# A hybrid decoder layer on eight cores: one program for all sequence positions becomes three, values are turned by DMA, and rope is done without DMAs

## The reference, cut to what matters

```
h = rms_norm(x, norm_gain)                    # x: (2, 4096, 2048)
proj = einsum('bsd,de->bse', h, w_in)         # 16384 columns: q, k, v (3072 each), z_attn, u_pool, z_pool, gates
q = rms_norm(q per head); k = rms_norm(k per head)     # heads of 128
for g, (window, dilation) in enumerate(((128, 1), (512, 4), (2048, 16))):   # 8 heads each
    qg, kg = partial_rope(q[g]), partial_rope(k[g])    # the first 32 of 128 dims, half-split pairing
    # query t attends to t, t-d, ..., t-window
    o_g, lse_g = dilated_window_attention(qg, kg, v[g], window, dilation)
attn = sum over g of softmax(lse)[g] * o_g             # i.e. sum of numerators / sum of denominators
y_attn = (attn * silu(z_attn)) @ w_branch_attn
pooled_g = (causal_mean(u_g, 2|4|8|16) - u_g) @ pool_maps[g]
y_pool = (pooled * pool_scale * silu(z_pool)) @ w_branch_pool
x + (sigmoid(gates_a) * y_attn + sigmoid(gates_p) * y_pool) @ w_out
```

## Time and profile before

| | |
|---|---|
| median of 3 runs | 1629.32 us (1627.96 to 1629.89) |
| span of the profiled execution, slowest core | 1627.1 us |
| spans of the eight cores | 1618.4 to 1627.1 us |
| PE busy | 1519.9 us, 93% |
| DVE, ACT, POOL busy | 663.1, 531.4, 202.2 us |
| mean granted PE clock of a core | 0.970 to 0.977 |
| moved by DMA | 158.85 MB, 98 GB/s on average |

### The profile page before, as it was taken

How to read it: one execution, slowest core, us unless ns; L and a number is a source line. 1 busy time by engine, 2 the same in 40 slices (tenths; PEclk the granted TensorE clock), 3 DMA queues, 4 the chain that set the end, 5 groups by cost and what they waited for, 6 DMA issues and landing times.

```text
span 1627.1 us, 22823 instructions; the slowest of 8 cores (1618.4 to 1627.1 us)
## 1 busy us (share of the span) xinstructions
PE 1519.9 (93%) x7774; PEld 751.7 (46%) x7774; DVE 663.1 (41%) x976; ACT 531.4 (33%) x880; POOL 202.2 (12%) x191
## 2 busy tenths in 40 slices
PE   2638999899999999989999999999999999999997
PEld 0203434344655555445555555565444444444443
DVE  4356339732100476666116677676322222112221
ACT  2324345333211556655236665621111111111000
POOL 1535463300000100000000000000000000000000
PEclk9859999999999999999999999999999999999999
DMA  9951544114443644343343443445344444444883
GB/s 196 200 152 50 140 125 134 51 49 88 97 112 52 110 99 73 85 95 75 75 77 63 105 104 60 78 73 100 69 77 75 74 76 77 78 78 78 191 209 106
DMA packets 77874, 158.85 MB, mean 98 GB/s; under 512 B 33536, under 2 KB 41600, under 8 KB 76992
## 3 DMA queue, kind: packets, MB, share of 16 engines
q0 software_dynamic: 20592, 84.42, 30.9%
q1 hardware_dynamic: 56544, 72.51, 14.6%
q10 hardware_dynamic: 624, 0.46, 0.2%
HBM read 216.27 MB, written 20.97 MB: 146 GB/s over the span
## 4 chain that ended last, share of the span: by engine, by line
PE 85%; DMA 4%; DVE 3%; issue 2%; POOL 2%; ACT 2%; SPq 0%; ACTq 0%; DVEq 0%; POOLq 0%
PE ps L725 64%; PE ps L1431 7%; PE ps L1381 7%; POOL s_acc L660 2%; DMA s_rota_76<-s_kst_72 2%; PE ps L742 2%; PE ps L1067 2%; PE ps L1102 1%; DMA s_xs_59<-xc 1%; ACT s_sqf L658 1%; PE ps L1106 1%; PE ps L848 1%; DMA s_rotb_101<-s_qS_100 1%; DVE s_rota_78 L775 1%; DMA s_rota_76<-s_kst_69 1%
## 5 line engine op out<-in xcount | busy, mean ns | idle before, releaser
L725 PE MATMUL ps<-s_hX,s_w_56 128*128 128x512 bf16 (+3 forms) x3712 | 799.4, 367 | 0.0
L725 PEld LDWEIGHTS ps<-s_hX,s_w_56 128*128 128x128 bf16 x3712 | 363.6, 98 | 373.5 <-issue 3.5
L587 POOL DMA_DIRECT2D s_w_56<-wst x140 | 74.1, 533 | 1206.3 <-PE ps L725 918.2
L725 PE MATMUL ps<-s_w_56,s_hX 128*128 128x512 bf16 x672 | 147.2, 379 | 0.0
L1431 PE MATMUL ps<-s_mT,s_w_56 128*128 128x512 bf16 x512 | 110.7, 379 | 0.0
L725 PEld LDWEIGHTS ps<-s_w_56,s_hX 128*128 128x128 bf16 x672 | 71.6, 107 | 71.5
L660 POOL TENSOR_TENSOR s_acc<-s_acc,s_sqf 128x1024 f32<-128x1024 f32 x35 | 85.9, 2455 | 127.6 <-ACT s_sqf L658 127.6
L1431 PEld LDWEIGHTS ps<-s_mT,s_w_56 128*128 128x128 bf16 x512 | 50.1, 98 | 60.4
L746 ACT ACTIVATE s_rr_51<-ps 128x512 f32<-128x512 f32 (+1 forms) x72 | 41.4, 576 | 103.6 <-PE ps L742 69.9
L751 DVE SCALAR_TENSOR_TENSOR s_kS_105<-ps,s_cst,s_rr_51 128x384 bf16<-128x384 f32 x8 | 4.9, 614 | 171.8 <-PE ps L725 167.0
L725 PE MATMUL ps<-s_hTh_55,s_w_56 128*128 128x512 bf16 x256 | 66.7, 406 | 3.6 <-DVE s_hTh_55 L695 2.4
(11 more groups left out here) (286 smaller groups left out, 1513.9 us busy)
## 6 DMA issues: line engine op xcount, KB each, us to landing
s_w_56<-wst POOLq DMA_DIRECT2D x136, 512.0 KB, 5.2
s_w_56<-wst POOLq DMA_DIRECT2D x4, 2048.0 KB, 16.6
s_w_57<-wst POOLq DMA_DIRECT2D x2, 2048.0 KB, 23.2
s_xs_58<-xc SPq DMA_DIRECT2D x6, 512.0 KB, 4.7
s_xs_59<-xc SPq DMA_DIRECT2D x6, 512.0 KB, 5.9
s_xs_60<-xc SPq DMA_DIRECT2D x6, 512.0 KB, 6.5
s_xs_61<-xc SPq DMA_DIRECT2D x6, 512.0 KB, 6.7
s_xs_62<-xc SPq DMA_DIRECT2D x6, 512.0 KB, 7.6
```

The lines of the kernel that those rows point to most:

```text
L587: yield ("dma", "pool", size * 1048576, lambda g: g.dma_start(out=t[:].rearrange("p k n -> p (k n)"), in_=src), first, bufs, dsem)
L725: yield ("op", "pe", mm_us(n), lambda t, kc=kc, a=lhs(kc), b=rhs(kc): t.matmul(ps[i][:, 0:n], lhsT=a, rhs=b, start=(kc == 0), stop=(kc == ...
```

## The change

1. **Three programs.** The sequence of 4096 is cut into 1184, 1024, 944 and 944 tokens. Core 0 of a sequence runs program a (no halo, no stage 1), the next b (halo of 16x74 = 1184 tokens), the last two c (16x128 = 2048). All three lie in one binary. Each engine reads a number from DRAM and enters its program by `If`. Pieces of own tokens are 400, 400, 384 in a, 512, 512 in b, 480, 464 in c.
2. **Stage 1** takes only the halo, in chunks by residue modulo 16: 370, 222, 222, 370 in b and 512, 256, 256, 512, 512 in c. Own keys and values of group 2 are projected in the head loop as those of groups 0 and 1. The 16 key and value weight blocks of group 2 are therefore loaded twice in b and c.
3. **Values feature-major.** `values` projects like keys, ACT copies to `vT`, and `v_turn` turns 128x128 tiles into `v0`, `v1`, `v2` by a transposing DMA on SP (9 to 10, 12, and 8 or 16 tiles a head for groups 0, 1, 2). Halo values are stored feature-major, and turned as they are loaded again.
4. **Rope without DMAs.** The weight columns are permuted so that the two halves lie on partitions 0 to 15 and 32 to 47. DVE reads one from the other's partitions: four operations.
5. **First loads.** Chunk 1 has eight x buffers of its own. The squares of chunk 0 have two buffers, and the process that squares runs ahead of the one that adds. DVE adds for chunks 0 and 2 in a and c, and for all but chunk 1 in b. `late_copy` is cut in four. Weight blocks wait for x loads at other points. Projections wait for x one 128-feature row at a time.
6. **Head loop.** Keys, values, queries, gate per head; group 2's denominators are summed on DVE ahead of the ones matmul, so a query column costs 5 columns of PE in all groups (6 before in group 2), 3 in a's group 2.

```diff
+class Kind:
+    def __init__(self, name, n, late, hl, halo, depth):
+        self.own = pieces(0, n)
...
+KINDS = [Kind("a", 1184, 0, 0, [], 8), Kind("b", 1024, 512, 74, [5, 3, 3, 5], 8),
+         Kind("c", 944, 512, 128, [4, 2, 2, 4, 4], 8)]
+CORES = [(b, k) for b in range(2) for k in (0, 1, 2, 2)]
+STARTS = [0, 1184, 2208, 3152]
...
+        def run(ename, eng):
+            r = eng.value_load(T["kind"][0:1, 0:1])
+            for i, S in enumerate(progs):
+                with eng.If(r == i):
+                    S.run(ename, eng)
...
+            if NH and k in (4, 6):
+                yield ("wait", E_x[(1 if k == 4 else 2, 7)])
+            if not NH and k in (3, 5):
+                yield ("wait", E_x[(1 if k == 3 else 2, 7)])
...
+            if c == 1:
+                xpos[(c, j)] = NXS + j
...
+    def sq_slots(c):
+        h = B_sqf
+        if c == 0:
+            return [(sqf, h), (sqfx, [B_sqfx])]
+        if 2 * kd.size[c] <= smax:
+            return [(sqf[:, smax * i:smax * i + smax], h[i:i + 1]) for i in range(2)]
+        return [(sqf, h)]
...
+            quick = c in (0, 2) or HL < 128 and c != 1
+            eng, dur = ("dve", dve_us(2 * m)) if quick else ("pool", 0.0024 * 2 * m)
...
+        for k in range(0, KC, 4):
+            src = hT[c][:, k:k + 4].rearrange("p k (r l) -> p k r l", l=HL)[:, :, :, HL - 32:HL]
+            dst = hL[:, k:k + 4].rearrange("p k (l r) -> p k r l", r=16)[:, :, r0:r1, :]
+            yield ("op", "pool", 0.0044 * 4 * 32 * (r1 - r0), lambda g, src=src, dst=dst: g.tensor_copy(
+                out=dst, in_=src), ...)
...
-            def swap(hf):
-                yield ("dma", "sp", 40e3, lambda s: s.dma_start(
-                    out=rb[32 + 16 * hf:48 + 16 * hf, 0:n], in_=st[16 - 16 * hf:32 - 16 * hf, 0:n]), [B_st], [Br[hf]],
-                    f"{tag}{ri}{hf}")
...
+        yield ("op", "dve", d, lambda v: v.tensor_tensor(
+            out=rb[0:32, 0:n], in0=st[32:64], in1=ts(32, 64), op=ALU.mult), [B_st, B_tab], [Br])
+        yield ("op", "dve", d, lambda v: v.tensor_tensor(
+            out=rb[32:64, 0:n], in0=st[0:32], in1=ts(0, 32), op=ALU.mult), [B_st, B_tab], [Br])
+        yield ("op", "dve", d, lambda v: v.tensor_tensor(
+            out=st[0:64], in0=st[0:64], in1=tc(0, 64), op=ALU.mult), [B_st, B_tab], [B_st])
+        yield ("op", "dve", d, lambda v: v.tensor_tensor(
+            out=st[0:64], in0=st[0:64], in1=rb[0:64, 0:n], op=ALU.add), [B_st, Br], [B_st])
...
+        jobs = [("lane", [0, 1, 2], [0]), ("k", [3], [0]), ("lane", range(4), [1]), ("lane", range(4), [2])]
+        jobs += [("k", [h], [0, 1, 2]) for h in range(4, 8)]
+        jobs += [("v", range(8), [0]), ("v", range(8), [1]), ("v", range(8), [2])]
+        for c in range(3, NH):
+            jobs += [("k", range(8), [c]), ("v", range(8), [c])]
...
+    def load_v(h, i):
+        yield ("dma", "sp", 524e3, lambda s: s.dma_start_transpose(
+            out=v2[i][:, 0:16, :], in_=v2d[h]), [B_v2d[(h, c)] for c in HALO], [B_v2[i]], f"lv{i}")
...
+    def v_turn(g, h, V, e, ti, tiles):
...
+        yield ("wait", e)
+        yield ("dma", "sp", 300e3, lambda s: s.dma_start_transpose(
+            out=vt[:, t0:t0 + tiles, :], in_=vT[ti][:, 0:128 * tiles]), [B_vT[ti]], [B_v], f"tv{g}{vi}")
...
+        yield ("wait", K["ev"])
+        yield ("wait", V["ev"])
...
+        for h in range(NHEAD):
+            for g in range(3):
+                K, Q, V = {}, {}, {}
+                yield from turns([keys(g, h, K), values(g, h, V), queries(g, h, Q)], not NH and (g, h) == (0, 0))
+                F.spawn(unit(g, h, K, Q, V), MID)
```

2324 lines of the change are left out of this document (1270 added, 1054 removed).

## The result

The changed kernel takes 1570.03 us (median of 5 runs, 1564.58 to 1596.58) against 1629.89: ratio 0.9624, 95% interval 0.9601 to 0.9646, so 3.8% faster. In some runs, whatever the kernel, the cores of one die or both show a lower clock and take some per cent longer; they are left out of every ratio, and e8, which has only two others (1543.12 and 1545.80 us), has no ratio. The forecast was 1484 us, 8.9% faster. The time is inside the range and on the right side, but the gain, 60 us, is less than half of the forecast 145. The profiled run took 1566.61 us; its slowest core, 3, runs program c and has a span of 1565.0. The four c cores have 1557.7 to 1565.0 (mean 1562.8), the b cores 1524.6 and 1528.0, the a cores 1488.1 and 1487.5. In what follows "c" is this mean over the four c cores of the profiled execution, and single rows are those of core 3.

What follows compares the result with a forecast made beforehand. TensorE, busy 93% of the span, was taken as the bound. For c: 1375.8 + 18.3 + 9 + 30 + 30 + 5 + 3 + 10.9 = 1482, with 2.2 more 1484 us; range 1455 to 1595.

Steps and rivals of the forecast that it cites:

- the prediction's prices: TensorE at 2.4 GHz: a matmul of 512 columns 215.6 ns, of 384 columns 162.5 ns, including 2.3 ns fixed.
- the end: Tail from TensorE's last result to the end of the span: 10.9 us, as before the change.
- Columns: TensorE's bf16 matmul columns in program c, counted as 3,302,016: 1375.8 us.
- Fixed price per matmul: On TensorE, 2.3 ns for each matmul besides its columns: 18.3 us for c's 7960.
- Turns: Stage 2's 24 transposing DMAs of values: 2.5 to 11.5 us each to landing, hidden, so no loss.
- the cover of 11.7: Stage 2: 11.7 us of queries, ones matmul and rope after a head's values, in which its turn can land unnoticed.
- Rivals 2 and 3: Stage 2: turns 1 to 5 us past cover, 1508 to 1604, middle 1545 (0.14); turns so slow the change loses (0.08).
- Start: Before the first projection at about 34 us: 30 us, with 4 gained on squares and 4 added for the program jump.
- Rest of stage 1: Stage 1 of c after the first projection: 30 us lost, bounds 5 and 79; rope exchange's 23.5 us wait removed.
- passage: From stage 1 to 2, first norms and the 448 KB table load: 5 us lost, bounds 0 and 13.
- Rival 1: Stage 1 keeps its loss, POOL holding DVE and four rope operations for three: 1533 us, chance 0.13.
- Signs named ahead: DVE near full from 45 to 110 us, PE full after 300; wrong if first projection past 40 or program a slowest.

Runs made afterwards that it cites:

- e8: Changed kernel with program c first in the chain, chunk 1's sum of squares after the first projections, big table ahead of halo reloads: profiled run 1543.12 us, no ratio.
- e6: Changed kernel with the first heads' halo reloads waiting until the big rope table has landed: ratio 0.9558 to the kernel before.
- e9: e8 with the token split moved to 1216, 1024, 928, 928: 1539.02 us, ratio 0.9443.
- e11: e8 with the stores of halo keys issued from ScalarE's queue in place of SyncE's: ratio 0.954.
- e12: e9 with the stores of halo keys issued from ScalarE's queue in place of SyncE's: 1538.28 us, ratio 0.9432.
- e15: e8 with all sums of squares added by VectorE, none by POOL: 1533.79 us, ratio 0.9349.
- e16: e8 with each x load of program c's chunks 4 to 7 a quarter of its width, result not kept: ratio 0.9442.
- e17: e15 with the first two heads' halo reloads put behind the first and second turn in SyncE's queue: 1517.02 us, ratio 0.9299.
- e1: Changed kernel with program c first and program a last in the chain of conditions: ratio 0.9676.
- e5: Changed kernel with halo key stores reading a rope table, so VectorE waits for no store; halo keys left out, a bound only: ratio 0.943.
- e18: Changed kernel with all sums of squares added by VectorE, none by POOL: 1525.68 us, ratio 0.9351.
- e14: e8 with halo key stores reading a rope table, so VectorE waits for no store; halo keys left out: 1521.67 us, ratio 0.9336.

## Why the prediction was off, point by point

The ledger of c after the change, core 3, by the prediction's prices: columns 1375.8, fixed 18.3, f32 sums 10.7, together 1404.8 of work. The first projection is at 43.82, of which 3.75 are counted: start 40.1. Up to 404 the matmuls counted in the trace are 269.1 of this work, in 404 - 40.1 = 363.9 us: 94.8 lost. 74.6 of them are idle; the rest is work that took longer than the price, in windows with a granted clock of 0.61 to 0.97. From 404 on TensorE is busy for 1146.7 (1145.15 and 1.54 in the last 12 us) where 1135.7 of work are left: 11.0 above the price. With 3.9 idle there and 10.5 at the end the sum is 1565.1.

- **Columns** (1375.8 and 7960 matmuls): the trace holds exactly these, 3,302,016 columns in 7960 bf16 matmuls, and the columns of a and b are as exact. f32 (9, measured 10.7) and the end (10.9, measured 10.5) were right within 2 us. So was the order of the programs, and that b and c both lie above a.
- **Fixed price per matmul** (2.3 ns): right for the long matmuls, and 9.9 us short in c's head loop. In a it is 24.0 short (busy 899.5 us from 100 to 1000 where the price gives 875.5). With 8.2 more at a's end (19.1 us after TensorE's last matmul, not 10.9) that is most of why a, forecast at 1451, took 1488. b, forecast at 1478 and measured at 1524.6 and 1528.0, was not taken apart.
- **Turns** (no loss): right. They land in 8.7 us, nearer to the forecast's upper bound (11.5) than to its lower one (2.5), and a pair of 13 to 14 us cost nothing in c, so the cover of 11.7 was counted short. Rivals 2 and 3 fell: no core of the changed kernel waits for a turn. Where the reloads go out in another place, some core does, once, in the first head: 2.8 to 24.4 us in the traces of e6, e8, e9, e11, e12, e15, e16 and e17. (Rival 2's middle of 1545 is not that of 1508 and 1604, which is 1556; nothing else rests on it.)
- **Start, 30 us:** it was 40. I bounded the jump over other programs by 0 and 5.5 us, and took 4. The first x load goes out at 2.53 us in the program that comes first, 5.83 in the second and 12.48 in the third. That is the jump: 10 us for the third, past the bound. Without it, in e1, the start is 28.4, where the forecast less its 4 has 26. The other side of it, that a program early in the chain is left later, stood in no term. It cost c nothing here (10.5 at the end), and is why e1 gained nothing from a start 11.7 us earlier.
- **Rest of stage 1, 30 us, and passage, 5:** together 94.8, 60 more than forecast and by far the largest miss. The passage is 7.6 of it by e6. The rest, some 87, is the step that failed. I took the loads as "just enough", by bytes over a rate: 105 us of transfer for 110 us. That supposes that the engines never stand still. They stood still for 17 us, since the weights are issued by an engine whose list had additions and copies first; then 9.4 MB came together, and small stores that VectorE and TensorE needed took up to 26.3 us among them. Taking the wait for these stores away gives 27 of the 60 us back (e5), taking the additions off POOL 45 (e18). The prediction read the row of the 23.50 us exchange, said that it was late for what lay ahead of it, and then took the wait away with the exchange. It should have asked which small DMA stands there next. POOL appeared in the sum only as an engine that holds VectorE, not as the issuer of the weights.
- **Rival 1** (1533, 0.13) came nearest in time and named the engine. Its mechanism, holds, is shown; whether it is the smaller part is not settled (e14 and e16 speak for it). Its remedy was the right one, and e18 with it ends at 1525.68.
- **Signs named ahead.** The first projection past 40 us was to show the forecast wrong, and came (43.8). VectorE was to be near full from 45 to 110; it was busy for some 52 of the 66 us from 44 to 110. TensorE was to be as full after 300 us as before; it was busy for 20.4 of 31 from 306 and 25.5 of 33 from 371.
- What is left between e15 (core 3, 1510.0) and the sum's 1482, by the same ledger: 45.3 us lost before 404 where 35 were forecast, 9.9 above the price after it, 7.4 more at the end since c is first there, 1.7 of f32, less 2 at the start. In stage 1 TensorE works 54 of 78 us between the first projection at 31.8 and 110 us (57.7 in the four windows up to 110, less 3.75 before the projection), part of it at a granted clock of 0.70 to 0.83.

On the two pages drawn on. By the Trainium skill (SBUF — State Buffer, "Who interferes with whom") VectorE and POOL lock a shared port pair; the rows agree for the bf16 rope operations (846 against 429 ns). The operation that reads PSUM and has one SBUF tile as input shows none of it (743 and 744), and that section leaves out instructions with at most one SBUF input. By the Trainium skill (Advanced Engine Details and Errata, "X-Bar Transpose (TRN2)") transposing DMAs run as fast as plain ones; the traces agree for the reload from DRAM (16 tiles, 512 KB, 4.9 us in the median, a plain key reload of 512 KB 4.8) and disagree for a turn within SBUF, which has fewer bytes and lands in 8.7 us.

## What to carry to other kernels

When a small DMA is late behind large loads, removing that DMA does not remove the place: find the next small DMA there, and who waits for it. Look for a stretch in which the DMA engines are idle just before one in which they are full; the loads that could have filled it are held in the list of an engine that computes. And before trusting a null result, look at the next narrow place: two edits here that moved stage 1 by 10 us each seemed worth little until the third opened the passage behind it. Where a core picks its program from a chain, look at both ends of the span: what is gained on entering is largely paid on leaving.

## What the hardware showed unexpectedly

A transposing DMA of 16 tiles kept SyncE for 2.5 us in the median, but for 21.7 us in e8, core 1, for 25.8 in e15, core 1, and for 29.1 in e11, core 5. In the stretch around the one of e15 the DMA engines of that core were nearly full and moved 67 GB/s:

```profile
DMA packets 5245, 3.03 MB, mean 67 GB/s; under 512 B 4741, under 2 KB 4741, under 8 KB 5243
...
q1 hardware_dynamic: 4821, 1.48, 98.7%
```

Two transposing reloads, two turns and 512 KB weight loads met there; the weights took 34.9 us to land, against medians of 5.2 to 6.3 in whole runs. Entering the second and third program of a chain of conditions cost about 3.3 and 10 us more than entering the first (first x load at 2.53, 5.83 and 12.48 us), and leaving the first and second about 7 to 9 and 3 us more than leaving the third (a 18.3 against 9.0, c 16.8 to 17.2 against 9.5, b as the second 12.4).
